# Overlong experts' rounds taken out of the pair loop and put behind it, and a twentieth 1 MB place for expert weights

## The reference, cut to what matters

```
sel    = softmax(x @ router_w) + router_b                 # 256 x 16
gbest  = the group of 4 experts with the best top-2 sum
idx    = the top 2 experts inside gbest                   # 2 experts for each token
h      = silu(x @ w_gate[e]) * (x @ w_up[e])              # 1024 -> 512
y      = sum over the two experts of gate * (h @ w_down[e])
```

## Time and profile before

| what | value |
|---|---|
| median of 3 runs | 716.07 us (714.9 to 716.73) |
| profiled execution, its own time | 717.58 us |
| its span in the trace | 715.9 us |
| PE busy | 695.5 us (97%), 5561 matmuls |
| PE weight loads busy | 420.9 us (59%) |
| DVE, ACT, POOL busy | 287.8, 231.9, 108.7 us |
| DMA | 246.22 MB, mean 344 GB/s |
| granted TensorE clock | 0.99 of 2.4 GHz |

### The profile page before, as it was taken

How to read it: one execution, slowest core, us unless ns; L and a number is a source line. 1 busy time by engine, 2 the same in 40 slices (tenths; PEclk the granted TensorE clock), 3 DMA queues, 4 the chain that set the end, 5 groups by cost and what they waited for, 6 DMA issues and landing times.

```text
span 715.9 us, 13946 instructions
## 1 busy us (share of the span) xinstructions
PE 695.5 (97%) x5561; PEld 420.9 (59%) x5562; DVE 287.8 (40%) x536; ACT 231.9 (32%) x435; POOL 108.7 (15%) x69
## 2 busy tenths in 40 slices
PE   9999999999999999999999999999799999999994
PEld 8989888864355335334389987876533523533532
DVE  5689937572112112012076765687111101111205
ACT  4565558151112112012174566625111111111202
POOL 2034100039100000000305000003910000000023
PEclk9999999999999999999999999999899999999998
DMA  9899335969999999999999634586989999999992
GB/s 319 289 385 374 122 114 192 380 242 422 418 422 422 421 421 422 421 423 420 412 388 389 243 119 156 209 322 242 422 356 422 404 424 421 422 423 421 422 419 92
DMA packets 51451, 246.22 MB, mean 344 GB/s; under 512 B 6265, under 2 KB 6610, under 8 KB 26834
## 3 DMA queue, kind: packets, MB, share of 16 engines
q1 hardware_dynamic: 51410, 245.65, 85.8%
HBM read 244.58 MB, written 1.05 MB: 343 GB/s over the span
## 4 chain that ended last, share of the span: by engine, by line
PE 87%; DVE 5%; DMA 3%; issue 2%; ACT 2%; POOL 0%; POOLq 0%; ACTq 0%; DVEq 0%
PE ps L2039 29%; PE ps L2053 15%; PE ps L1829 12%; PE ps L1824 10%; PE ps L2020 4%; PE ps L2001 4%; DMA weights<-in_moe_w_up 3%; PE ps L1779 3%; DVE ring_lo L1170 2%; PE ps L1757 1%; PE ps L2009 1%; PE ps L2175 1%; DVE scratch L1321 1%; ACT xT L836 1%; PE ps L1864 1%
## 5 line engine op out<-in xcount | busy, mean ns | idle before, releaser
L2039 PE MATMUL ps<-weights,scratch 128*32 128x512 f32 (+1 forms) x1792 | 197.4, 593 | 0.8 <-DMA weights<-in_moe_w_up 0.7
L2039 PEld LDWEIGHTS ps<-weights,scratch 128*32 128x32 f32 x1792 | 61.8, 110 | 130.6 <-issue 129.5
L2053 PE MATMUL ps<-weights,scratch 128*32 128x512 f32 (+1 forms) x1024 | 114.6, 594 | 0.4 <-issue 0.2
L1170 DVE TENSOR_TENSOR ring_lo<-weights,w_hi 128x2048 fp32r<-128x2048 f32 x36 | 83.5, 2332 | 16.2 <-ACT w_hi L792 15.7
L1624 DVE TENSOR_TENSOR scratch<-ps,scratch 128x512 f32<-128x512 f32 x16 | 11.1, 691 | 176.5 <-PE ps L2039 176.5
L792 ACT ACTIVATE w_hi<-weights 128x2048 fp32r<-128x2048 f32 x35 | 66.7, 1914 | 29.5 <-PE ps L1829 15.7
L2053 PEld LDWEIGHTS ps<-weights,scratch 128*32 128x32 f32 x1024 | 32.7, 110 | 70.3 <-issue 70.0
L1636 DVE SCALAR_TENSOR_TENSOR rounded<-ps,gslot,rounded 128x512 fp32r<-128x512 f32 x32 | 24.0, 750 | 93.4 <-ACT rounded L1041 93.4
L740 POOL TENSOR_TENSOR scratch<-rounded,gate_of 128x256 f32<-128x256 f32 x14 | 8.6, 616 | 290.4 <-PE ps L2193 289.5
L1041 ACT ACTIVATE rounded<-ps,gslot 128x512 fp32r<-128x512 f32 x32 | 22.0, 688 | 90.2 <-PE ps L2053 90.2
L1003 ACT ACTIVATE scratch<-ps,ln_col 128x256 f32<-128x256 f32 (+1 forms) x40 | 19.3, 540 | 98.1 <-PE ps L2020 92.7
(11 more groups left out here) (277 smaller groups left out, 958.5 us busy)
## 6 DMA issues: line engine op xcount, KB each, us to landing
weights<-in_moe_w_gate SPq DMA_DIRECT2D x64, 1024.0 KB, 11.7
weights<-in_moe_w_down SPq DMA_DIRECT2D x64, 1024.0 KB, 12.6
weights<-in_moe_w_up SPq DMA_DIRECT2D x48, 1024.0 KB, 14.9
scratch<-in_moe_w_up SPq DMA_DIRECT2D x16, 1024.0 KB, 18.4
weights<-in_a_w_in SPq DMA_DIRECT2D x15, 1024.0 KB, 13.5
weights<-in_kv_w SPq DMA_DIRECT2D x8, 1024.0 KB, 14.9
weights<-in_a_w_out SPq DMA_DIRECT2D x4, 1024.0 KB, 15.2
weights<-in_b_w_q SPq DMA_DIRECT2D x4, 1024.0 KB, 14.5
```

What stands on the lines that cost most here:

```text
L1170: V.tensor_tensor(low_part(i), ring[:, piece_slot(i), :, :], w_hi[:, i % HI, :, :].bitcast(F32), ALU.subtract).then_inc(lo_ready, 1)
L2039: last = mm(ps[rows, bank, :], own[:, HALF_K * part + k, rows], w, start=part == 0 and k == 0, stop=part == 1 and k == HALF_K - 1)
L2053: last = mm(ps[rows, bank, :], hT[:, 2 * part + k, rows], w, start=part == 0 and k == 0, stop=part == 1 and k == 1)
```

## The change

1. The overflow code leaves the pair loop. On PE, ACT and DVE one `overflow()` stands behind the loop; one register `rounds` for the layer replaces the counts of the pairs, so the loop has no `value_load` of a count and no `If` for it. The rounds of all experts run one after another. Their weights are not those of the ring: SP loads six chunks for each round into the spare places and two others (`load_overflow`). On PE the code has no variants for first and second expert.
2. SP waits no more for `o_read` and `o_free` in its loads and sums up no counts.
3. `TWICE` is 8: the odd pairs have a place of their own for the eighth chunk too, in `scratch` at 38 K. `LAST_UP` is gone; `NEXT_UPS` has four chunks. Pair 1's eighth chunk is loaded together with its sixth, while the mixer runs. Room comes from small tiles that now share a buffer `early` with ones that are dead by then (`seg`, `lam_in`, `lam_p` with `silu`, `pick_g`, `put`), and from overflow tiles that share with `xe`.
4. The routing's last part on DVE computes the list of rounds with 9 small instructions where it had 7.
5. PE's matmuls on zeros between the layers are 60 where they were 79; ACT's `high(A_PIECES + 1)` stands behind `rounded_and_whole(2)`.

```diff
-TWICE = 7
+TWICE = 8
-        LATE = (0, 46 * K)
-        late = [at(first, HALF_K, COLS) for first in LATE] + [last_place]
+        LATE = (CHUNK_SIZE, CHUNK_SIZE + 46 * K, 0, CHUNK_SIZE + 38 * K)
+        late = [tail[:, first:first + CHUNK_SIZE].rearrange("p (k n) -> p k n", k=HALF_K) for first in LATE]
...
+            def load_overflow(layer):
+                sp.wait_ge(slots_ready, layer + 1)
+                count = sp.value_load(rounds[0:1, 0:1], min_val=1, max_val=ROUNDS)
+                with sp.If(count > 1):
...
                 sp.wait_ge(*chunk_read(PAIRS * layer + pairs, matrix, part))
-                if (matrix, part) != (GATE, 1):
-                    sp.wait_ge(o_free if matrix == DOWN else o_read, finished)
...
-            NEXT_UPS = ((UP, 0, BOTH), (UP, 1, (0,)))
-            LAST_UP = ((UP, 1, (1,)),)
+            NEXT_UPS = ((UP, 0, BOTH), (UP, 1, BOTH))
...
                     if c == 10:
                         load_chunk(layer, 1, 1, UP, 0, 1)
+                        load_chunk(layer, 1, 1, UP, 1, 1)
...
-                sp.wait_ge(slots_ready, layer + 1)
                 for p in range(1, PAIRS):
-                    count_overflow(p - 1)
                     if p == 1:
...
-                        order = NEXT_GATES[1:] + NEXT_UPS + LAST_UP + DOWNS
+                        order = NEXT_GATES[1:] + NEXT_UPS + DOWNS
                     elif p < 3:
-                        order = NEXT_GATES + NEXT_UPS + LAST_UP + DOWNS
+                        order = NEXT_GATES + NEXT_UPS + DOWNS
                     elif p < 5:
-                        order = LAST_UP + NEXT_GATES + DOWNS + NEXT_UPS
+                        order = NEXT_GATES + DOWNS + NEXT_UPS
                     elif p < PAIRS - 1:
-                        order = LAST_UP + DOWNS + NEXT_GATES + NEXT_UPS
+                        order = DOWNS + NEXT_GATES + NEXT_UPS
                     else:
-                        order = LAST_UP + DOWNS
+                        order = DOWNS
...
# DVE (ACT alike), behind the pair loop
+                overflow()
+                dve.wait_ge(o_free, done)
...
# ACT
                 if layer == 0:
                     high(A_PIECES)
-                    high(A_PIECES + 1)
...
             rounded_and_whole(2)
+            high(A_PIECES + 1)
...
# PE, in the pair loop
                     into_hidden(BANK_A, two, odd, GATE, gate_ps, who)
                     pe.wait_ge(slots_ready, layer + 1)
-                    count = pe.value_load(chunks[0:1, bass.ds(i, 1)], min_val=0, max_val=ROUNDS + 1)
                     into_hidden(BANK_B, two, odd, UP, up_ps, who)
-                    overflow(count, two, odd, i, pair, done)
...
# PE, behind the loop
                 for t in range(TT):
                     add_up(t, (1,)).then_inc(acc_ps, 1)
+                overflow(layer)
...
-            for _ in range(79):
+            for _ in range(60):
                 nothing(BANK_A, COLS // 4)
             turn_normed()
```

More of the change, by code:

```diff
@@ L106, in build @@
             pass
+        K = 256
+        with nc.sbuf_tensor("before_tail", [P, (RING + SPARE) * CHUNK_SIZE], F32R), \
+                nc.sbuf_tensor("tail", [P, CHUNK_SIZE + 54 * K], F32) as tail:
+            pass
         weights = sb("weights", [P, RING + SPARE + 1, HALF_K, COLS])
@@ L133, in build @@
         iota = sb("iota", [P, T])
-        seg = sb("seg", [P, 2 * T])
+        with nc.sbuf_tensor("early_r", [P, 4 * K], F32R) as early_r:
+            pass
+        early = sb("early", [P, 4 * K])
+        seg = early[:, 0:2 * T]
         ident16 = sb("ident16", [P, P], BF16)
@@ L261, in build, with o_weight @@
         o_gslot = sb("o_gslot", [P, 1])
-        xr_hi = carve(TT, D, home=rounded)
-        assert place[0] == 46 * K
+        o_weights = [spare[:, c, :, :] for c in range(SPARE)] + late[1:3]
+        def o_weight(matrix, part):
+            return o_weights[2 * matrix + part]
         ps = ctx.enter_context(nc.psum_tensor("ps", [P, 8, COLS], F32))
@@ L455, in chunk_places @@
         def chunk_places(layer, odd, c):
[L457 to L460, removed]
+            if odd and SPARE <= c < TWICE:
+                return tail, *LATE[c - SPARE:c - SPARE + 2]
+            first, other = ((RING + i if odd and i < TWICE else chunk_slot(layer, i)) * CHUNK_SIZE for i in (c, c + 1))
             return weights[:, :, :, :].rearrange("p s k n -> p (s k n)"), first, other
@@ L520, in load_chunk @@
                              w.rearrange("one (p k) n -> p (one k n)", p=P)).then_inc(arrived, 16)
[L522 to L527, removed]
+            done = sp.alloc_register("sp_done")
+            sp.reg_mov(done, 1)
+            def load_overflow(layer):
+                sp.wait_ge(slots_ready, layer + 1)
+                count = sp.value_load(rounds[0:1, 0:1], min_val=1, max_val=ROUNDS)
+                with sp.If(count > 1):
+                    sp.wait_ge(yd_ps, PAIRS * (layer + 1))
+                    with sp.Fori(1, count, 1) as r:
+                        e = sp.value_load(round_e[0:1, bass.ds(r - 1, 1)], min_val=0, max_val=E - 1)
+                        sp.wait_ge(o_free, done)
+                        for matrix in range(3):
+                            for part in range(2):
+                                w = experts[matrix]
+                                rows = w.shape[2] // 2
+                                w = w[layer, bass.ds(e, 1), part * rows:(part + 1) * rows, :]
+                                sp.dma_start(o_weight(matrix, part).rearrange("p k n -> p (k n)"),
+                                             w.rearrange("one (p k) n -> p (one k n)", p=P)).then_inc(o_in, 16)
+                        sp.reg_add(done, done, 1)
             def load_small():
@@ L1558, in route @@
[L1558 to L1562, removed]
+                more, upto = count_f[0:1, 1, :], count_f[0:1, 3, :]
@@ new lines, in route @@
+                step(V.tensor_tensor_scan(upto, ones[0:1, 0:E], more, 0.0, ALU.mult, ALU.add))
+                V.tensor_scalar(rounds[:, :], upto[:, E - 1:E], 1.0, None, ALU.add)
+                nth = iota[0:1, 0:ROUNDS]
+                sums = upto.unsqueeze(1).to_broadcast([1, ROUNDS, E])
+                step(V.tensor_tensor(ended, nth.unsqueeze(2).to_broadcast([1, ROUNDS, E]), sums, ALU.is_gt))
+                step(V.reduce_sum(expert_f, ended, axis=AX.X))
+                step(V.tensor_tensor(ended, ended, sums, ALU.mult))
@@ L1620, in experts @@
                         pick_two(2 * two + 1)
-                    overflow(count, done, i)
                     dve.wait_ge(up_ps, 2 * pair + 2)
```

234 lines of the change are left out of this document (105 added, 129 removed).

## The result

The changed kernel takes 708.84 us (median of 4 runs, 708.66 to 710.35), the kernel before 716.38 beside it (714.9 to 716.73): a ratio of 0.9899, 95% interval 0.9872 to 0.9926, or 7.5 us. The forecast was 709.4. Medians and ratios in this document leave out one slow execution each of e4 and e10, of 4026.6 and 2499.8 us, whose cause stays open. The profiled execution is the longest of the four, 710.35 us, with a span of 708.5; of before it was 717.58 with 715.9. So the difference of the spans to explain is 7.4 us.

What follows compares the result with a forecast made beforehand. PE (87% of the chain, with gaps at the overflow branch) and the weight stream were taken as bounds; 2.4 + 5.4 + 0.6 - 0.25 = 8.15 off 717.58 gave 709.4 us, range 706.5 to 714.5.

Steps and rivals of the forecast that it cites:

- The two large terms: Gains forecast in the two MoE layers: 2.4 us in layer 0 and 5.4 us in layer 1.
- The place, layer 0: Layer 0's MoE: one chunk loaded earlier into the twentieth place lets the last down product start sooner; gain 2.4 us.
- Both layers end on the stream, with PE hardly behind it: Step: last down products start 0.16 and 0.09 us idle after the weights, so removing PE's gap alone brings little.
- The bound of 2.5: Layer 0's upper bound: if more PE gaps go, including pair 1's down product, the stream holds the gain at 2.5 us.
- Layer 1: Layer 1's MoE: without PE's gap and slow clock, the stream with the extra chunk allows 693.0 for 698.4; gain 5.4 us.
- Against the median it is 6.7.: Whole kernel: gain is 6.7 us against the median 716.07, as layer 1's gap is probably often shorter than profiled.
- Branch behind the loop on PE: PE's skip over the moved overflow code, once a layer: costs 0.3 us, the low end of the gaps seen.
- the slower rival: Branch behind the loop misses its code on PE and DVE, 4.08 us each: 719.0 us, chance 0.07.
- Between the layers: Layer 0 to 1: fewer matmuls on zeros and ACT's earlier root bring the transposes forward; gain 0.6 us.
- DVE's branch at the end: Register load and branch before bn_stats on DVE delay layer 1's end: -0.25 us.
- The gaps are not the overflow code's: Rival: the first pass fetches loop code whatever stands in it, so PE's gaps move elsewhere: 716.2 us, chance 0.12.
- The place brings nothing: Rival: the extra chunk gains layer 0 nothing and layer 1 only its dry stretch, 2.9 us: 714.3 us, chance 0.13.

Runs made afterwards that it cites:

- e4: Changed kernel with PE's count read and branch over 155 never-run matmuls (about 310 instructions) put back in the pair loop; 721.14 us, ratio 1.0052.
- e10: Changed kernel with pair 1's first gate chunks loaded in two halves, the first 1.7 us earlier; 709.79 us, ratio 0.9914.
- e1: Changed kernel again, no edit; 708.52 us, ratio 0.9885.
- e11: Changed kernel once more, no edit, beside the kernel with the earlier stream; 708.74 us, ratio 0.9903.
- e2: Changed kernel without the twentieth place (TWICE 7, load order of before), overflow code still behind the loop; 713.69 us, ratio 0.9953.
- e3: Kernel before with PE's overflow branch and code left out of the loop, 19 places; 714.86 us, ratio 0.9972.
- e5: Changed kernel with the same put-back branch over 155 never-run matmuls, run again for its profile; 717.8 us, one execution.
- e6: Changed kernel with a put-back branch in PE's loop over 50 never-run matmuls (about 100 instructions); 709.27 us, ratio 0.9917.
- e9: Changed kernel with 79 matmuls on zeros between the layers instead of 60; 710.94 us, one execution.
- e7: Changed kernel with the overflow code behind the loop left out on PE, DVE and ACT; 708.82 us, one execution.
- e8: Changed kernel with ACT's rounding of the second piece in front of the root again; 709.46 us, one execution.

## Why the prediction was right

709.4 was forecast and 708.84, 708.52 and 708.74 came. The two large terms are the right mechanism with nearly the right size; the small ones failed in both directions. The gain is 7.5 us by the medians of the result, 6.8 beside e1 and 7.0 beside e11, where 6.7 was forecast. The terms sum to 8.15; the distances gained 9.3 of the profiled execution, and its late start took 2.0 of that, so that a part of the close agreement is chance.

- *The place, layer 0: 2.4 forecast, 2.68 measured.* The step "Both layers end on the stream, with PE hardly behind it" holds, and e2 is the proof: 2.5 us a layer without the place. I had PE come at 352.8, beside the stream's 352.7. In fact pair 1's loss of 1.2 us, which I had left in, went too, so PE came early and waited 0.96 us for its last up chunk. The bound of 2.5 that I gave for that case was the term. The loss stands in before's chain, where pair 1's down product takes 8.16 us (197.24 to 205.40), the others that wait for nothing 7.00:

```profile
197.24 2.71 PE ps L2053 x22
199.94 0.14 issue
200.09 4.88 PE ps L2053 x41
...
205.40 13.73 PE ps L2039 x125
```

- *Layer 1: 5.4 forecast, 5.59 measured.* No gap, clock at 1.00 where it was 0.51, the last down product 198.99 us after the start of the MoE (199.1 forecast), after a wait of 1.04 us (about 1 forecast).
- *"Against the median it is 6.7."* The comment that the gap in layer 1 is often shorter, and "takes from the gain and not from the time after", is borne out by e3: the spread of before was the branch's. By the medians: code out of PE's loop alone 715.35 - 714.86 = 0.5 (by the means 1.6); e2 against e3, mostly the work between the layers (138.71 against 137.66 us), 1.2; the place 5.2. Read from the profile alone one would have credited the code with more, for its execution lay above the median. Nor need the 5.2 be the place's own: with a long skip put back the time was 721.1, above before. In the two profiled executions PE loses 11.5 us to gaps and half clock in e5 and 9.4 in before (1.24 + 0.27 + 1.16 + 4.08 + 2.64), and the two layers together take 406.9 and 406.2 us: with long gaps the place shows no gain. With the old branch and short gaps, its usual case, the place was not tried.
- *Branch behind the loop on PE: 0.3 taken.* Nothing in the three profiles of the changed kernel, 0.3 in e6, 1.6 in e9 and in e10. The low end of the bounds was the right choice, but gaps like those of the slower rival exist: about 1.6 us each time, not 4.08. The zeros hide none of it: in e10, with 60 of them, the transposes come 12.53 us behind the last down product, 1.6 later than in e1.
- *Between the layers: 0.6 forecast, 0.8 to the transposes and 1.0 to the next MoE measured.* The forecast's own numbers, 366.3 for about 367.0 (the earlier trace rows has 367.09), give 0.7 to 0.8 and not 0.6. The costs taken for the branches, 0.3 on PE and 0.25 on DVE, did not come (e7). On ACT I counted no branch, and there it has one: its 0.68 idle would have made the old order 1.1 us late (e8), so moving the rounding was worth 1.1 and not 0.4. With 10.95 us from the last down product the transposes start where DVE's row lets them.
- *DVE's branch at the end: -0.25 forecast, 0 measured.* It is there (0.35 us from the last work of the pair to bn_stats, where I said 0.8, had 0.09), but the second pair of bn_stats, which I had 0.2 to 0.3 late, still waits for PE:

```profile
696.66 1.30 DVE L1664 BATCH_NORM_STATS2 stats<-ps 128x6 f32<-128x512 f32 x2 [0.35 <-PE ps L2142]
698.21 1.30 DVE L1664 BATCH_NORM_STATS2 stats<-ps 128x6 f32<-128x512 f32 x2 [0.25 <-PE ps L2019]
```

- *The rivals.* "The gaps are not the overflow code's" falls with e3 and e6. Its argument, the wait inside pair 1's down product, was real but wrongly read: pair 1 has its own branch, 3 us ahead of that product, and without the branch the loss is gone (in e3 the next gate product starts 6.9 us behind the start of this down product, in e1 7.0). So the branch's loss lies at it and a few us behind it: 0.27 us at pair 1's branch in before, and the 1.2 in the down product. "The place brings nothing" falls with e2.

The Trainium skill (Runtime: NRT & Kernel Launch, section Instruction fetch mechanics) puts the stall on a taken branch out of the fetched window. The runs agree in kind: about 310 instructions passed over stall PE, about 100 don't in the one profile taken.

## What to carry to other kernels

When an engine's gaps and a transfer stream end within a microsecond of each other, work out both floors before removing either: here taking out the gap alone was worth 0.5 us by the medians, and one more buffer on top 5.2, while e4, with the buffer and long gaps, was slower than before. A stall that comes from fetching code varies between executions, so its size is read from the spread of many runs and not from one profile; keep rarely used code out of a loop's body and let it stand behind it. And when such code moves, its branch lands on every engine: look on each for the first instruction behind it that someone waits for.

## What the runs showed of the hardware

- Skipped code costs by chance: 0 to 6 us a run for the same kernel (before, 25 runs), idle pieces of 0.14 to 4.08 us in the first pass of the loop and none in later passes (before and e5). Some 100 instructions cost nothing, some 310 did. Why one execution pays and the next does not stays open; so does the difference between e4's median of 721.1 and e5's 717.8, which e4's own range includes.
- The granted clock fell to 0.50 (1.2 GHz) after idles of only 2.21 and 1.90 us in e5, and stayed there for 3.4 us; after one of 2.06 in the same trace it did not fall. In the kernel before it fell 3.1 us into an idle of 4.08 (at 510.9) and stayed for 6.9. A stall of 2 us thus cost nearly 4 in two of three cases.
- Starting the stream 1.7 us earlier with 1 MB transfers split into halves gave nothing over both layers: 366 against 377 GB/s in its first 10.5 us, the last up chunk 0.4 us later in layer 0 and 0.4 earlier in layer 1.
